# New fill counts, item order and engine assignments in a two-layer RWKV-7, Mamba-2 and differential attention encoder

## What is computed

```python
mod = (c_act @ ada_w[l] + ada_b[l]).reshape(bsz, N_SUB, 3, D_MODEL)
h = modulated_norm(x, norm_w[l, 0], mod[:, 0])
x = x + 0.5 * mod[:, 0, 2, None] * rmsnorm(swiglu(h, ffn_w13[l, 0], ffn_w2[l, 0]), norm_w[l, 1])
```

```python
proj = h @ w_in
y_r, v_first = rwkv7_branch(p_r, *rwkv_params, v_first, vres)
y_m = mamba2_branch(p_m, *mamba_params)
y_d = diff_attention_branch(p_d, lam_vecs, subln_w, lambda_init)
g = jax.nn.sigmoid(p_g).reshape(bsz, s, N_BRANCH, D_MODEL)
merged = g[:, :, 0] * (y_r @ w_br_r) + g[:, :, 1] * (y_m @ w_br_m) + g[:, :, 2] * (y_d @ w_br_d)
return merged @ w_out, v_first
```

## Time and profile before

| | us |
|---|---|
| median of 3 runs | 2737.57 (2735.68 to 2737.82) |
| profiled execution | 2737.22 |
| its span in the trace | 2735.5 |
| PE busy | 2620.0 (96%) |
| DVE busy | 1413.6 (52%) |
| ScalarE busy | 499.4 (18%) |
| POOL busy | 232.0 (8%) |
| share of the chain that ended last: PE, DVE, ScalarE, issue, DMA | 81%, 11%, 3%, 2%, 2% |

### The profile page before, as it was taken

One profiled execution on the slowest core, in us unless ns is written; L12 is line 12 of the kernel. 1 busy time (PEld: TensorE's weight loads), 2 busy tenths in 40 slices (PEclk: granted clock), 3 DMA queues, 4 the chain that ended last, 5 costly groups with the idle time before them and its releaser, 6 DMA issues.

```text
span 2735.5 us, 66483 instructions
## 1 busy us (share of the span) xinstructions
PE 2620.0 (96%) x30077; PEld 1906.3 (70%) x30077; DVE 1413.6 (52%) x2560; ACT 499.4 (18%) x1016; POOL 232.0 (8%) x372
## 2 busy tenths in 40 slices
PE   6999999999999999999999999999999899999999
PEld 6777877777775555577787778777778745546776
DVE  3552465677775856312035425456787768562001
ACT  1000223122222332100010011322222223221000
POOL 6000102000001101100000010110000011100000
PEclk9999999999999999999999999999999999999999
DMA  9894433322327542484469734423222275424452
GB/s 364 309 337 151 133 117 123 111 83 92 116 80 239 169 168 94 144 291 165 157 242 340 271 128 142 152 91 113 87 83 88 91 253 191 143 96 154 138 168 93
DMA packets 226348, 445.12 MB, mean 163 GB/s; under 512 B 7545, under 2 KB 102327, under 8 KB 226065
## 3 DMA queue, kind: packets, MB, share of 16 engines
q1 hardware_dynamic: 211376, 395.59, 41.5%
q0 software_dynamic: 12960, 38.98, 4.5%
q10 hardware_dynamic: 1728, 6.29, 0.6%
HBM read 422.88 MB, written 17.96 MB: 161 GB/s over the span
## 4 chain that ended last, share of the span: by engine, by line
PE 81%; DVE 11%; ACT 3%; issue 2%; DMA 2%; POOL 1%; DVEq 0%; ACTq 0%; SPq 0%; POOLq 0%
PE ps L1039 79%; DVE scratch L2228 5%; DVE scratch L2231 2%; DVE scratch L2234 1%; DVE gbc L2234 1%; PE ps L1068 1%; DVE scratch L2544 1%; DMA scratch<-in_ada_w 1%; DMA ring<-in_w_in 1%; DMA scratch<-acs_scratch 0%; DMA acs_scratch<-scratch 0%; ACT scratch L2053 0%; ACT scratch L2051 0%; ACT scratch L2200 0%; DVE x L2234 0%
## 5 line engine op out<-in xcount | busy, mean ns | idle before, releaser
L1039 PE MATMUL ps<-hT,ring 64*64 64x256 f32 (+3 forms) x9472 | 1147.9, 367 | 8.3 <-issue 3.1
L1039 PEld LDWEIGHTS ps<-hT,ring 64*64 64x64 f32 (+2 forms) x9472 | 943.0, 160 | 155.9 <-issue 35.8
L1039 PE MATMUL ps<-scratch 64*64 64x32 f32 (+6 forms) x15264 | 846.7, 255 | 56.8 <-DVE scratch L2228 16.1
L1039 PEld LDWEIGHTS ps<-scratch 64*64 64x64 f32 (+2 forms) x15264 | 592.6, 140 | 332.3 <-issue 206.2
L2228 DVE TENSOR_TENSOR scratch<-scratch,ps 128x256 f32<-128x256 f32 (+3 forms) x314 | 155.2, 494 | 661.1 <-ACT scratch L1895 533.1
L1039 PE MATMUL ps<-ring,hT 64*64 64x256 f32 (+2 forms) x2816 | 425.4, 421 | 5.3 <-DVE scratch L2234 2.6
L1039 PEld LDWEIGHTS ps<-ring,hT 64*64 64x64 f32 (+1 forms) x2816 | 228.7, 149 | 143.3 <-issue 116.8
L2228 DVE TENSOR_TENSOR scratch<-scratch 128x512 f32<-128x512 f32 (+4 forms) x426 | 276.1, 648 | 75.4 <-ACTq L2035 31.8
L1039 PE MATMUL ps<-ring,scratch 128*128 128x512 f32 x512 | 234.7, 593 | 0.5
L2234 DVE SCALAR_TENSOR_TENSOR scratch<-scratch,ccol 128x1024 f32<-128x1024 f32 x120 | 154.2, 1285 | 15.2 <-DMA scratch<-in_ada_w 11.3
L1895 ACT ACTIVATE scratch<-ps 128x512 f32<-128x512 f32 x40 | 23.9, 597 | 746.1 <-PE ps L1039 746.1
(11 more groups left out here) (228 smaller groups left out, 1392.8 us busy)
## 6 DMA issues: line engine op xcount, KB each, us to landing
ring<-in_w_in SPq DMA_DIRECT2D x56, 2048.0 KB, 9.0
ring<-in_ffn_w SPq DMA_DIRECT2D x88, 1024.0 KB, 9.0
scratch<-in_ada_w SPq DMA_DIRECT2D x35, 2048.0 KB, 16.2
scratch<-in_ffn_w SPq DMA_DIRECT2D x44, 1024.0 KB, 5.0
ring<-in_w_branch_mamba SPq DMA_DIRECT2D x8, 2048.0 KB, 8.0
scratch<-acs_scratch POOLq DMA_DIRECT2D x24, 512.0 KB, 5.8
scratch<-fill_scratch SPq DMA_DIRECT2D x16, 512.0 KB, 8.7
ring<-in_w_branch_rwkv SPq DMA_DIRECT2D x4, 2048.0 KB, 11.1
```

What stands on the lines that cost most here:

```text
L1039: return pe.matmul(o, lhsT, rhs, start=start, stop=stop)
```

## The change

1. `FILL` has another order, in which c items alternate with others sooner, and `FILL_PAIR` other counts. The sum stays 448. The last pair has eight steps at its `end`, where it had none.
2. The first conv item's taps move from pair 2 to pair 1 (none in one direction, four in the other, three per level); the others stay where they were.
3. ScalarE's `conv_sigmoid` is put between an item's evacuation and its scaled copies, if an item is due there; items filled up to `lv` are taken ahead of it.
4. POOL computes the group norm's power ahead of the next pair's weight loads, and the product of the fourth z item moves by one pair.
5. In the heads, a fourth product stands behind each o but the last head's. The order of the 32 difference products is new: those that need the last head come last. DVE's merges are split into pieces of 512 columns, placed inside the bodies of heads 2, 3, 5 and 6.
6. The out projection's first weights are loaded in two parts, the first of them earlier.
7. ScalarE copies the parameters at the start and issues the loads of the down weights.

The core of the diff; of the table of counts, two of eight rows stand here:

```diff
-FILL = [("z", 0), ("z", 1), ("z", 2), ("z", 3), ("c", 0), ("q", 0), ("c", 1), ("q", 1), ("c", 2), ("q", 2),
-        ("c", 3), ("q", 3), ("c", 4), ("c", 5), ("v", 0), ("v", 1)]
+FILL = [("z", 0), ("z", 1), ("z", 2), ("c", 0), ("z", 3), ("c", 1), ("q", 0), ("c", 2), ("q", 1), ("c", 3),
+        ("q", 2), ("c", 4), ("q", 3), ("c", 5), ("v", 0), ("v", 1)]
...
-FILL_PAIR = ((8, 8, 8, 2, 2, 2, 2, 0, 2, 0, 1, 1, 4, 1, 2, 0, 2, 2, 3),
-             (14, 10, 10, 3, 3, 3, 3, 0, 2, 0, 1, 1, 4, 1, 2, 0, 2, 2, 3),
...
-             (14, 8, 7, 1, 2, 2, 2, 0, 1, 0, 1, 1, 3, 1, 1, 0, 1, 1, 0))
+FILL_PAIR = ((7, 9, 9, 1, 2, 2, 2, 0, 2, 0, 1, 2, 6, 1, 2, 0, 2, 1, 2),
+             (13, 8, 8, 0, 0, 1, 1, 0, 1, 0, 1, 1, 6, 1, 2, 0, 1, 1, 3),
...
+             (13, 7, 8, 1, 1, 1, 1, 0, 2, 0, 2, 2, 7, 2, 2, 0, 2, 2, 8))
...
-CONV_AT_LEVELS = CONV_SIGMOID = {2: 0, 3: 1, 4: 2, 5: 3, 6: 4, 7: 5}
...
+CONV_AT_LEVELS = CONV_SIGMOID = {1: 0, 3: 1, 4: 2, 5: 3, 6: 4, 7: 5}
...
-                def down_weights(j):
-                    parity = j % 2
-                    if j >= 2:
-                        sp.wait_ge(*down_done(l, f * FJ + j - 1))
-                    w2 = row(a["ffn_w2"], l)[:, f, j * 256:(j + 1) * 256, :].rearrange("a (k p) n -> p (a k) n", p=P)
-                    sp.dma_start(w2s[:, parity, :, :], w2).then_inc(w2_loaded[parity].sem, 16)
...
+                sp.wait_ge(*bm_part(l, 5))
+                sp.dma_start(out_slot[:, 0:6, :], kmaj(w_o[:, 0:6 * P, 0:512])).then_inc(slot_loaded[IT_OUT % 2].sem, 16)
+                sp.wait_ge(*group_done(l, group_of(IT_OUT - 2) + 1))
+                sp.dma_start(out_slot[:, 6:8, :], kmaj(w_o[:, 6 * P:8 * P, 0:512])).then_inc(slot_loaded[IT_OUT % 2].sem, 16)
+                load(l, IT_OUT + 1, (IT_OUT + 1) % 2, kmaj(w_o[:, :, 512:1024]), free_after=group_of(IT_OUT - 1) + 1)
...
                 for q in range(2, PAIRS):
+                    group_norm_rstd(q - 2)
                     next_pair(q)
-                    group_norm_rstd(q - 2)
-                    if q == 2:
+                    if q == 3:
...
+                    late = KT - 1
+                    first = [(0, k, t) for k in range(late) for t in range(TT)] + [(1, k, 0) for k in range(late)]
+                    behind = [(0, late, 0), (0, late, 1), (1, late, 0)] + [(1, k, 1) for k in range(KT)]
...
-                    beside(3 if h == 0 else 2)
+                    beside(4 if last else 3 if h == 0 else 2)
...
-                    beside(4 if h == 0 else 3)
+                    beside(3 if last else 4)
...
+                def down_weights(j):
+
+                    w2 = row(a["ffn_w2"], l)[:, f, j * 256:(j + 1) * 256, :].rearrange("a (k p) n -> p (a k) n", p=P)
+                    act.dma_start(w2s[:, j % 2, :, :], w2).then_inc(w2_loaded[j % 2].sem, 16)
+
+                down_weights(0)
+                down_weights(1)
...
+                    if j:
+                        act.wait_ge(*down_done(l, f * FJ + j))
+                        down_weights(j + 1)
...
+            act.wait_ge(*params_turned(0, 1))
+            act.activation(prm[:, :], ps[:, 3, :], ACT.Identity).then_inc(params_evac.sem, 1)
...
+                    if between is not None:
+                        conv_sigmoid(between)
...
-                        fill_evacuations(q - 1, "k3")
-                        if q - 1 in CONV_SIGMOID:
-                            conv_sigmoid(CONV_SIGMOID[q - 1])
+                        fill_evacuations(q - 1, "lv")
+                        fill_evacuations(q - 1, "k3", CONV_SIGMOID.get(q - 1))
...
-                    read_params(0, 3)
                     first_sum(1)
+                    dve.wait_ge(*params_evac(0, 1))
...
-                        if p in CONV_AT_LEVELS:
+                        if p in CONV_AT_LEVELS and p > 1:
...
-                            convolve(2 if d else 4)
+                            convolve((4 if d else 0) if p == 1 else (2 if d else 4))
...
-                            convolve(2)
+                            convolve(3 if p == 1 else 2)
...
+                    if h == 6:
+                        mamba_added(1, 0)
...
+                    if h in (2, 3):
+                        mamba_gated(0, h - 2)
+                    if h == 6:
+                        mamba_gated(1, 1)
...
-                    if h == 5:
-                        merge(IT_BM, 1, 2, sg_second, (0,))
...
+                gated_rows(IT_BD, 1, 2, sg_first, 0, 0)
+                own.step(added_rows(sg_first, 0, 0))
+                gated_rows(IT_BD, 1, 2, sg_first, 1, 0)
+                raised(added_rows(sg_first, 1, 0), hT_ready(l, 3))
+                gated_rows(IT_BD, 1, 2, sg_first, 0, 1)
+                evacuated(l, added_rows(sg_first, 0, 1), out_group - 2)
+                merged_to_channels(0)
+                gated_rows(IT_BD, 1, 2, sg_first, 1, 1)
+                evacuated(l, added_rows(sg_first, 1, 1), out_group - 1)
```

More of the change, by code:

```diff
@@ L161, in loads_before @@
 def loads_before(item, parity):
-    return sum(2 if n in FFN_ITEMS else 1 for n in range(item) if n % 2 == parity)
-CONV_AT_LEVELS = CONV_SIGMOID = {2: 0, 3: 1, 4: 2, 5: 3, 6: 4, 7: 5}
+    return sum(2 if n in FFN_ITEMS or n == IT_OUT else 1 for n in range(item) if n % 2 == parity)
+CONV_AT_LEVELS = CONV_SIGMOID = {1: 0, 3: 1, 4: 2, 5: 3, 6: 4, 7: 5}
 C_CONVW, C_V0 = 0, 120
@@ L656, in feed_forward @@
                         conditioning(l + 1, j - 2)
-                    down_weights(j)
             for l in range(DEPTH):
@@ new lines, in difference_products @@
+                        if (k, t) == (0, 0):
+                            pe.wait_ge(*slot_loaded[par](l, loads_before(item, par) + 1))
+                            bank_free(l, g)
+                        if h == 0 and t == 0:
+                            pe.wait_ge(*yd_ready(l, k + 1))
+                        if (h, k, t) == (1, KT // 2, 1):
+                            pe.wait_ge(*hT_ready(l, 3))
+                            turn_tile(0, merged).then_inc(merged_turned.sem, 1)
+                        ins = mm(ps[:, 2 * (g % 2) + t, :], ydT[:, k, t * P:(t + 1) * P], slot(par)[:, k, :],
+                                 k == 0, k == KT - 1)
@@ L2933, in _, with gated_rows, added_rows, mamba_gated @@
                 own.restart()
+                def gated_rows(first, ks, b, gates, h, t):
+                    gg = group_of(first + h * ks)
+                    if t == 0:
+                        dve.wait_ge(*gate_ready(l, 2 * b + h + 1))
+                        dve.wait_ge(*(rows_done(l, 4) if (b, h) == (2, 1) else group_done(l, gg + 1)))
+                    elif (b, h) == (2, 1):
+                        dve.wait_ge(*group_done(l, gg + 1))
+                    gated = gates[:, h, t, :]
+                    own.step(tt(gated, gated, ps[:, 2 * (gg % 2) + t, :], ALU.mult))
+                def added_rows(gates, h, t):
+                    dst = merged[:, t, h * 512:(h + 1) * 512]
+                    return tt(dst, dst, gates[:, h, t, :], ALU.add)
+                def mamba_gated(h, t):
+                    gated_rows(IT_BM, 2, 1, sg_second, h, t)
+                def mamba_added(h, t):
+                    ins = added_rows(sg_second, h, t)
+                    if t == 0:
+                        own.step(ins)
+                    else:
+                        evacuated(l, ins, group_of(IT_BM + 2 * h))
                 def head_bias(h):
```

91 lines of the change are left out of this document (35 added, 56 removed), and 10 rows, old and new, of the table FILL_PAIR.

## The result

The changed kernel took 2743.78 us (median; single executions lie between 2733.07 and 2754.69), the kernel before 2736.81 (2730.49 to 2742.70) beside it. The ratio is 1.0025, 95% interval 1.0014 to 1.0037: slower by a quarter of a per cent, where 2713 was forecast. The profiled execution took 2744.34 us, with a span of 2742.6.

A forecast was written before the change was run, and what follows sets the result against it. PE bounds the kernel, so gains come only from its 115 us of idle time and half-clock stretches. Pairs -8.4, clock -3, heads -10 and start -3 sum to -24.4, from 2737.6 to 2713; range 2698 to 2731.

The forecast's parts named there:

- the tables: Fill steps moved in the RWKV pairs: per layer -7.0, +0.3, +5.8 and +2.5; -3 for the clock over both layers.
- the wait at u0: Pairs 2, 3 and 6: sigmoid ahead of ScalarE's copies ends DVE's delay, 3 x -2.07 = -6.2 per layer, bounds -6.2 and 0.
- The levels: Points lv, k0 to k3 of the pairs: fewer fill steps there give -7.0 us per layer, between -7.5 and -6.
- There the removed steps buy nothing, and PE idles: Levels of pairs 4 to 7: stay at 3.08 us, held by DVE's taps, so the change there is 0.
- credited the clock with 3 us elsewhere: Behind the last pair: with PE's 3.18 us gap gone the clock stays up, -1.5 per layer, -3 for two.
- rival (c): Emptied levels of pairs 1, 2, 4 to 7: 12 stretches at half clock, up to 3.4 us each, 2754; chance 0.07.
- (1): End of the last pair: eight steps, 3.46 us of work in 3.18 of idle time, cost +0.3 per layer.
- (2): Between r0 and y of a pair: 31 steps, 13.4 us with 7.6 hidden, cost +5.8 per layer, bounds +4 and +9.
- (3): Turns between pairs: four more steps, five turns 15.4 to 16.4, others 19.8 at most; +2.5 per layer, bounds +1 and +4.
- this delay: DVE work beside POOL's z product, moved into pair 2: a whole delay would give back 1.5 us per layer.
- Heads and start: Heads: PE's waits for normed o and Mamba merges go, -10.0 in all; start: conditioning sum ends earlier, -3.0.

The follow-up runs named there:

- the four zero steps per layer: Changed kernel plus one step of zero-operand matmuls, adding nothing, at each of k0 and k1 of pairs 1 and 4: 2735.6 us, ratio 0.9991.
- in pairs 1 and 2 alone: Changed kernel plus zero-operand steps, up to two at each of k0 to k3, in pairs 1 and 2 only: 2746.8 us, ratio 1.0042.
- everywhere: Changed kernel plus zero-operand steps wherever k0 to k3 have fewer than two, 30 more per layer: 2740.0 us, ratio 1.0010.
- the old tables: Changed kernel with item order, fill counts and taps' pairs of before: 2721.3 us, ratio 0.9941; with eight steps at the last pair's end, also 2721.3.
- the heads alone: Kernel before with only the heads' part of the change: 2726.5 us, ratio 0.9969.
- the start alone: Kernel before with only the start's part, ScalarE copying the parameters: 2735.0 us, ratio 0.9989.

## Why the prediction was wrong

The forecast of 2713 missed by 31. Two terms make all of it: the tables, 21.5 (22.5 measured, +1.0 in the working: 2 x (-7.0 + 0.3 + 5.8 + 2.5), rounding, and -3 of clock), and the wait at u0, 9.1. The terms' own bounds, added up at their ends, give 2701 to 2751 and not the 2698 to 2731 that the prediction draws from them, but none of them has room for a clock that falls in the levels.

**The levels, and the clock: the step that failed.** "There the removed steps buy nothing, and PE idles" was right for the pace: a level of pair 4 lasts 655.54 - 652.46 = 3.08, as forecast. What it left out was a price for the idle time: it put the clock of the emptied levels at nothing, and credited the clock with 3 us elsewhere. The levels were to give 7.0 per layer. From a pair's last small product to its first copy r they took 6.9 and 1.6 more: the stretch ahead of the first level gave 4.3 and 3.2 (forecast 2.4), but the levels themselves took 10.2 and 4.8 more where 4.7 less were forecast. Of the tables' 22.5 us about 15 are clock, my estimate from (43.9 - 13.6) x 0.5. The mechanism is that of rival (c), to which I gave 0.07. That it named 12 stretches and 12 falls came is chance: ten were in pairs that it named, two of these in pair 5, where the clock fell before too, and pair 6 had none. Its size was off the other way: I priced a us of half clock at half a us, and the executions show 0.28 (0.55 x 0.5); that part of it falls where PE waits for DVE anyway is my reading, not shown. So its 2754 was too dear and its chance too small. My reason against it, "a pair's last level already runs without a step", was the wrong example: one such level between full stretches is not several in a row. The Trainium skill, "TensorE: Matmul & The Clock Gate", section "A second HAM failure mode: psum-queue depth-cycling", says that frequent micro-idles between groups of matmuls made the clock swing; the trace agrees, with falls to 0.50 in levels where the longest gaps are waits of 0.7 to 1.2 us for DVE, in a kernel whose PE is busy for 96% of the span, and with the four zero steps per layer that took 12.5 us off the lost clock.

**What lets the clock fall.** Two things go with the falls. Empty points: in pairs 1 and 4, where k0 and k1 have no step, the clock fell in both layers without any long gap (489.3, 656.5 and in the second layer 1844.4, 2011.6); a zero step at each helped, though one at each didn't hold the clock in pair 1. Gaps named "issue" in a sparse level: six of the 12 falls begin within 2 us of one. PE's row in pair 2:

```profile
551.69 1.27 PE L1029 MATMUL ps<-scratch 64*64 64x32 f32 x60
556.17 1.75 PE L1029 MATMUL ps<-scratch 64*64 64x32 f32 x30 [3.21 <-issue]
```

In the second layer gaps of 2.35 (1905.9), 1.03 (2064.6) and 2.46 (2177.8) stand the same way; before, only pair 5 had it. These gaps come in every kernel; the table decides where they fall. That PE should be fuller around them was not shown one by one: zero steps left the half clock of pair 2 at 13.7 us when they stood in pairs 1 and 2 alone, and at 6.8 when they stood everywhere. Two falls are of another kind. The one in the turn behind pair 1 follows PE's wait of 2.15 us shown below. The one at 1738.5 is ahead of the second layer's levels, where kernels with the old tables have one too (1724.3 with the heads alone, 1729.6 with the start alone). And the start ran at 0.50 in some of the profiled executions and not in others with the same code there: that part is open.

**Where the 43 steps go.** (1) The eight at the end did what was said (no wait, clock 1.00 at 843.7), but the same in the kernel with the old tables shows no gain, and there PE waits for ScalarE instead. (2) The steps between r0 and y were forecast with u0 at about 0 per layer (5.8 - 6.2); from a pair's first copy r to its group norm the pairs measured -0.2 and -3.0. With u0 giving less, the steps there cost less than the 5.8. (3) The turns were to cost 2.5 and cost 6.9 and 6.6 per layer, between the same operations as in the earlier trace rows. The turns into pairs 5 and 6 take 19.7 and 20.3 us in the changed kernel (15.5 and 16.9 before, forecast 17.7 to 19.8), that into pair 2 19.2 (17.3 before, forecast 15.4 to 16.4). The turns before add up to 117.5 us, so with these figures the working's bounds should have been -5 and +4, not +1 and +4. PE's waits for L2239 in the turns grew from 1.6 to 6.4 us. In the turn from pair 1 to pair 2, DVE and POOL of the changed kernel:

```profile
526.37 6.09 DVE L2239 TENSOR_TENSOR scratch<-scratch 128x512 f32<-128x512 f32 x5
...
529.82 2.35 POOL L920 TENSOR_TENSOR scratch<-scratch 128x1024 f32<-128x1024 f32 x1
...
532.61 0.62 PE L1029 MATMUL ps<-stack_i,scratch 64*64 64x64 f32 x14 [2.15 <-DVE scratch L2239]
```

The kernel with the old tables has the same five operations without the product:

```profile
528.61 3.32 DVE L2239 TENSOR_TENSOR scratch<-scratch 128x512 f32<-128x512 f32 x5
```

2.77 us more, again 6.09 at 1879.45 in the second layer, and PE stands behind them. The working's upper bound for this delay was a whole one of 1.5; the delay was 1.5 beside one operation before, and is 2.8 beside five, on the path. The rule named there (the Trainium skill, "GPSIMD Engine Reference", section "8. Key points") holds, and was the case to price at more than its old size. In the turns into pairs 5 and 6 the 22 steps in a row, the taps and the order of items share the growth; their parts were not told apart.

**The wait at u0.** 3 x 2.07 per layer was right for the wait, which is gone, and wrong for what was late next. A gap named "issue" lay inside it, hidden: while PE waited for DVE it stood anyway. So 3.3 of 12.4 us came (5 by the ratios). The bound 0 was in the range; the term should have stood nearer to it, since PE has such gaps throughout: 14 in the kernel before, 18.9 us in all, the longest in the earlier trace rows.

**Heads and start** came as reckoned, -10.0 and -3.4 (forecast -10 and -3.0). Before, PE's wait at L1756 stood in the last two heads (first line; the line number of before); in the changed kernel the same transposes of the last head (L1750) have none. The first long matmuls begin at 35.52, where they began at 37.53 before:

```profile
1096.19 0.66 PE L1756 MATMUL ps<-ident,scratch 128*128 128x128 f32 x4 [1.57 <-DVE scratch L2234]
...
1109.87 0.60 PE L1750 MATMUL ps<-ident,scratch 128*128 128x128 f32 x4
...
35.52 6.67 PE L1029 MATMUL ps<-hT,ring 128*128 128x128 f32 x44 [1.58 <-ACT hT L1836]
```

They and u0 make the 17 us of the kernel with the old tables: 10.0 + 3.4 + 3.3, in which some 3 us are clock (lost 13.6 for 19.2).

## What to carry to other kernels

In this kernel filler work between small dependent matmuls held the clock as well as filling time: before moving it away from a place where the engine waits anyway, price the clock of what is left, above all where several waits would stand in a row with nothing between them. A wait's length is what a change can give only if nothing else was hidden in it; look for the gaps that the profile gives no releaser for. And a table of counts is judged by where item ends, side engines' products and such gaps come to lie, not by its sum.
